# A transformer block on one core: in the FFN's second product, the sixth product's right blocks are loaded ahead of the last two left operands

## What is computed

```
FFN_HIDDEN = int(math.ceil(8 * D_MODEL / 3 / 256)) * 256        # 2816

def swiglu(h, w_in_ffn, w_out_ffn):
    g, u = jnp.split(h @ w_in_ffn, 2, axis=-1)
    return (jax.nn.silu(g) * u) @ w_out_ffn

xl = xl + gt2 * swiglu(modulate(rms_norm(xl, g_ffn[l]), sh2, sc2), w_ffn_in[l], w_ffn_out[l])
...
return rms_norm(xl, g_final)
```

## Time and profile before

| | us |
|---|---|
| three timed runs | 1302.32, 1302.75, 1305.46 |
| median | 1302.75 |
| the profiled execution's own time | 1297.05 |
| its span in the trace | 1295.2 |
| TensorE busy | 1255.0 (97% of the span) |
| DVE, ACT busy | 923.3 (71%), 652.1 (50%) |

### The profile page before, as it was taken

The page is one execution under the profiler, slowest core; times in us unless marked ns, Lnnn a source line. Parts: engine busy times, 40 slices in busy tenths (PEclk is TensorE's granted clock), DMA queues, the critical chain, the costliest instruction groups (busy, mean ns, idle before and its releaser), DMA issues. The chain is left out here.

```text
span 1295.2 us, 22622 instructions
## 1 busy us (share of the span) xinstructions
PE 1255.0 (97%) x7808; PEld 656.8 (51%) x7808; DVE 923.3 (71%) x1546; ACT 652.1 (50%) x1240; POOL 305.3 (24%) x301
## 2 busy tenths in 40 slices
PE   8999999999898999999999999999999999999997
PEld 1564656444675666665455444444444444444443
DVE  3779986686688999974356976666666676576387
ACT  2532123544697999993125554444454444312225
POOL 0100000121132789960001233333322230000001
PEclk9999999999999999999999999999999999999999
DMA  9627702052240131011112222222223204997953
GB/s 372 241 89 301 292 33 65 1 163 66 74 174 1 34 130 32 0 34 49 49 49 82 65 85 71 71 75 81 89 89 89 74 31 135 325 341 270 358 194 131
DMA packets 106709, 158.89 MB, mean 123 GB/s; under 512 B 8209, under 2 KB 67089, under 8 KB 104849
## 3 DMA queue, kind: packets, MB, share of 16 engines
q1 hardware_dynamic: 106640, 158.00, 35.6%
HBM read 135.95 MB, written 19.93 MB: 120 GB/s over the span
## 5 line engine op out<-in xcount | busy, mean ns | idle before, releaser
L1105 PE MATMUL PS<-arena 128*128 128x512 f16 (+9 forms) x7208 | 1206.6, 327 | 21.3 <-DMA arena<-in_w_mod 7.2
L1105 PEld LDWEIGHTS PS<-arena 128*128 128x128 f16 (+3 forms) x7208 | 605.9, 102 | 592.9 <-issue 47.5
L2708 DVE SCALAR_TENSOR_TENSOR arena<-arena 128x512 f16<-128x512 f32 x148 | 120.9, 823 | 76.7 <-ACT arena L2010 76.7
L2010 ACT ACTIVATE arena<-arena 128x512 f16<-128x512 f32 x140 | 87.6, 629 | 130.4 <-PE PS L1105 130.4
L2615 DVE TENSOR_REDUCE arena<-PS 128x1 f32<-128x512 f32 (+1 forms) x160 | 105.5, 680 | 9.8 <-PE PS L1105 9.8
L2122 ACT ACTIVATE arena<-arena 128x512 f16<-128x512 f32 x77 | 48.2, 629 | 127.4 <-DVE arena L2856 72.8
L1946 ACT ACTIVATE arena<-PS 128x512 f16<-128x512 f32 x144 | 91.3, 634 | 2.6 <-PE PS L1105 2.1
L980 POOL TENSOR_TENSOR arena<-arena 128x2 f32<-128x2 f32 (+1 forms) x18 | 21.1, 1173 | 260.9 <-DVE arena L2467 260.9
L1020 POOL TENSOR_TENSOR arena<-arena 128x512 f16<-128x512 f32 x64 | 74.0, 1158 | 23.7 <-ACT arena L1949 22.4
L1072 POOL TENSOR_TENSOR arena<-arena 128x512 f32<-128x512 f32 x20 | 26.4, 1322 | 222.8 <-DMA arena<-in_w_ffn_in 212.0
L2635 DVE TENSOR_TENSOR arena<-PS,arena 128x512 f16<-128x512 f32 x96 | 65.4, 682 | 8.3 <-ACT PS L1949 8.3
(11 more groups left out here) (199 smaller groups left out, 1111.2 us busy)
## 6 DMA issues: line engine op xcount, KB each, us to landing
arena<-in_w_ffn_out SPq DMA_DIRECT2D x121, 256.0 KB, 5.0
arena<-in_w_mod SPq DMA_DIRECT2D x24, 1024.0 KB, 7.3
arena<-in_w_ffn_in SPq DMA_DIRECT2D x88, 256.0 KB, 2.9
arena<-in_w_in SPq DMA_DIRECT2D x9, 1024.0 KB, 5.3
left_operands<-arena SPq DMA_DIRECT2D x33, 256.0 KB, 2.2
arena<-left_operands SPq DMA_DIRECT2D x3, 2816.0 KB, 14.9
arena<-lay_bias SPq DMA_DIRECT2D x4, 1536.0 KB, 8.9
arena<-in_x SPq DMA_DIRECT2D x2, 2048.0 KB, 14.7
```

Of the source, the lines that this page charges most:

```text
L1105: return pe.matmul(out, lhsT, rhs, start=start, stop=stop, skip_group_check=True)
L2010: act.activation(aS[n % RING][:, 0], weight_block(p, b), ACT.Copy, scale=WS).then_inc(blk_hi, 1)
L2708: dve.scalar_tensor_tensor(dst[:, 1], src, WS, dst[:, 0], ALU.mult, ALU.subtract).then_inc(blk_lo, 1)
```

## The change

P3's eleven right blocks (steps 5 x KQ to 6 x KQ - 1) are loaded ahead of the left operands. The first eight, as many as there are raw slots, come ahead of S4; the other three come between S4 and A22, which is now the last. SP waits for the stored sums and P6's splits at its old place, behind S4. Nothing else is changed.

```
             load_fo(3 * KQ + 4, 5 * KQ)
             sp.wait_ge(fo_mm, 4 * (DOWN.index("P6") + 1))
             load_x2("C21")
+            load_fo(5 * KQ, 5 * KQ + FO_RAW)
             load_left(KEPT_OUT.index("S4"))
             for j in range(4):
                 sp.wait_ge(t2_out[j], 16 * len(range(j, KQ, 4)))
             sp.wait_ge(fo_lo, 3 * KQ)
+            load_fo(5 * KQ + FO_RAW, 6 * KQ)
             load_left(KEPT_OUT.index("A22"))
-            load_fo(5 * KQ, 7 * KQ)
+            load_fo(6 * KQ, 7 * KQ)
```

## The result

| | before | after |
|---|---|---|
| median of 20 timed runs, us | 1302.18 | 1305.79 |
| lowest to highest | 1298.60 to 1305.46 | 1302.87 to 1310.36 |
| profiled execution, us | 1297.05 | 1302.87 |
| its span | 1295.2 | 1301.1 |

The ratio is 1.003 with a 95% interval of 1.0021 to 1.004: the changed kernel is slower by 3.6 us. One or two executions of each of four kernels further down took 1340 to 4666 us, and the ratios and medians leave them out. The prediction had 3.8 us more and a time of 1306.5. The sum was right. Two of its terms were far too small, and their errors cancelled.

The account below looks back on a forecast made before the run. The prediction took TensorE, busy 97% of the span, to bound the kernel. Its terms 3.9 - 1.3 + 1.2 = +3.8 us, added to the median of 1302.75, gave 1306.5 us, with a range of 1302.0 to 1310.0.

Parts of the forecast that it names:

- wait for A22: At P3's start TensorE, ready at 1229.3, waits until about 1233.2 for A22 on the count shared with S4: +3.9 us.
- clock behind it: After TensorE's wait at P3 the granted clock falls to 0.57 over 4 us: +1.2 us, bounds 0 and 1.7.
- waits that go: P4's waits for DVE's splits vanish because DVE is earlier and has 7 us of cover: -1.3 us.
- so its waits cost 1.3 us: In the kernel before, P4 would end undisturbed at 1286.5 but ends at 1287.77, a loss of 1.3 us.
- ready at 1229.3: TensorE is ready for P3's first matmul at 1229.3, 3.5 us after A22's old landing at 1225.8.
- TensorE doesn't wait there: In the kernel before, TensorE has no wait at P3's first matmul, which stands at 1229.3.
- the second product was the same there: The timed runs' median lies 5.7 us above the profiled execution, with the second product the same, so the difference is added.
- price per block: Each of P3's blocks takes 0.66 us of the DMA engines, so eleven land A22 7.3 us later.
- SP's issue backs up: Rival: the three blocks between S4 and A22 hold SP, A22 is issued at about 1226; +5.6 us, 1308.4; 13%.
- P4's waits stay: Rival: DVE isn't earlier after all, so P4 still waits for splits; +5.1 us, 1307.9; 7%.
- the clock doesn't fall: Rival: TensorE's clock stays up after the wait at P3; +2.6 us, 1305.3; 22%.
- A22 comes in time: Rival: A22 lands by 1229.3, so TensorE doesn't wait at P3 and only -1.3 us is left, 1301.4; 8%.

Follow-up runs that it names:

- before, again: The kernel before, with no edit, run once more for a second trace: ratio 1.000 (0.9987 to 1.0014), median 1301.77 us.
- before, own count: The kernel before, with its order of loads kept but A22 taken off S4's semaphore count: ratio 0.9994 of before (0.9981 to 1.0008).
- changed, again: The changed kernel, with no edit, run once more for a second trace: ratio 1.0025 of before (1.0012 to 1.0038).
- three blocks last: The changed kernel with A22 loaded ahead of P3's last three blocks, shared count kept: ratio 1.0019 of before (1.0006 to 1.0031), median 1303.46 us.
- changed, own count: The changed kernel with A22 off S4's semaphore count, so P3 waits for S4 alone and P4 for A22: ratio 0.9961 of before (0.9946 to 0.9976).
- the same, again: The changed order with A22 off S4's count, run once more on another chip: ratio 0.9963 of before (0.9949 to 0.9977).
- S4 first, own count: The changed kernel with A22 off S4's count and S4 loaded ahead of all eleven blocks: ratio 0.9965 of before (0.9953 to 0.9977).
- wait kept warm: The changed kernel with 30 extra matmuls on zero weights ahead of P3's wait: ratio 1.0009 of before (0.9993 to 1.0026).

## Why the prediction was right, and which terms were not

The mechanism was right in the steps that the traces can show. A22 lands behind the eleven blocks, 20.9 and 20.6 us behind C21 (21.0 by the prediction's count). P3 waits for an operand that it doesn't read, the clock falls (already within the wait, not only behind it), DVE is earlier, P4's gaps go, and the end is TensorE's.

The sizes of the terms:

| term | predicted | measured |
|---|---|---|
| wait for A22 | +3.9 | +7.6 and +6.9 (two traces) |
| clock behind it | +1.2 (0 to 1.7) | +1.3 and +1.5; 2.7 behind the gap of 3.3 us |
| waits that go | -1.3 | -5.1 and -4.8 (the ratios 0.9961 and 0.9963 of the order without a wait); 4.9 lost in the second trace of before |
| sum | +3.8 | +3.6 |

The failed step is in the first part, "so its waits cost 1.3 us", and in the third, "ready at 1229.3" against a landing worked out from the same trace. So is "TensorE doesn't wait there", of P3's start: it waited 1.03 and 2.02 us there in the two other traces of this order. All of them take one distance from one trace: C21 landed 17.2 us ahead of P3's due time. In the other traces it was (lost is TensorE's end less the due time less 57.2 us; where there is no gap, the due time is counted back from the end):

| trace | C21 lands | P3 due | distance | gaps of TensorE in P3 and P4 | lost |
|---|---|---|---|---|---|
| before | 1212.1 | 1229.3 | 17.2 | 0.7 | 1.3 |
| before, again | 1216.7 | 1231.1 | 14.4 | 4.1 | 4.9 |
| before, own count | 1218.1 | 1231.5 | 13.4 | 3.0, and the clock | 5.3 |
| changed | 1214.3 | 1227.6 | 13.3 | 7.6, and the clock | 9.0 |
| changed, again | 1217.7 | 1231.3 | 13.6 | 6.9, and the clock | 8.5 |
| three blocks last | 1215.0 | 1231.8 | 16.8 | 3.3, and the clock | 6.2 |
| changed, own count | 1216.2 | 1232.1 | 15.9 | none | 0 |
| the same, again | 1217.5 | 1231.1 | 13.6 | none | 0 |
| S4 first, own count | 1218.4 | 1231.2 | 12.8 | none | 0 |
| wait kept warm | 1211.7 | 1229.4 | 17.7 | none, 30 more matmuls | 6.5 (these matmuls) |

A shorter distance makes both kernels slower. In the order of before P3's and P4's splits are late, and the loss rises from 1.3 to 4.9 and 5.3 us. With the shared count and the new order the gap is the time from C21 to A22 less the distance (20.9 - 13.3, 20.6 - 13.6, 20.1 - 16.8). Hence each of the two terms was 3 to 4 us too small, and their difference held. That the errors have opposite signs follows from the one distance in both; that they are so nearly equal was luck, for the prediction didn't foresee it. The losses give the result again: 9.0 and 8.5 less 4.9 is 4.1 and 3.6 us.

The prediction noted that its profiled execution was 5.7 us below the median and then said that the second product was the same there. This was the sentence to test. The spans of the two traces of before differ by 5.5 us: 3.6 are lost in P3 and P4, and by 1.8 TensorE reaches P3 later, which was lost ahead of the second product, as it has no gap from 1000 to P3 in either trace. Why C21 lands at another distance from run to run was not tried; the waits for P5's and P7's blocks ahead of it differ (DVE's idle time before the sums of P6, P5 and P7 is 30.6 us in the first trace of before and 32.4 in the second), and that is all the traces say.

The wait's own range, 3.6 to 5.5, missed both traces of the changed kernel. The range for the whole, 1302.0 to 1310.0, held. The price per block is less firm than one trace made it look: over the five traces with eleven blocks and S4 ahead of A22 it is 20.6 to 22.2 us from C21 to A22, which with operands of 7.0 and 6.7 leaves 0.63 to 0.77 us per block, and 0.80 where eight stood ahead of it. The 0.60 us that the prediction set beside its 0.66 lies below all of these. Two slips of arithmetic changed nothing: its shares for slower add up to 45% and more (25, 13, 7), not 43%, and A22's landing by the terms of the rival with SP's issue is 1226.1 + 1.2 + 6.7 = 1234.0, not 1234.4; no row stands behind its 1.2 and 1.3.

Of the rivals, that SP's issue backs up didn't happen (A22 was issued at 1218.10 and landed 17.1 us later, of which its own transfer takes 6.7, so it stood ten microseconds in the queue); that P4's waits stay is out; that the clock doesn't fall is out; and that A22 comes in time is out.

## What to carry to other kernels

Before a load is moved behind others, look at who waits on its semaphore, not only at who reads its data: with a shared count the first reader waits for the last load. An order of loads and the waits that hang on it are one edit; here each alone was worth nothing or less, and both together 0.4%. And take a wait from more than one execution where the profiled one lies outside the timed ones: its slack is then not the usual slack.

## What the runs showed of the chip

How long the granted clock stays low behind a wait was not what the trace of before had led me to expect. A gap of 1.03 us left it at 1.00, one of 2.02 us was followed by (0.13 + 0.30) x 8 = 3.4 us at 1.2 GHz, and with gaps of 3.3, 6.9 and 7.6 us it was low for 6.8 us each time. With a long wait most of the low stretch falls into the wait and costs 1.3 to 1.5 us; with the gap of 3.3 us it falls behind it and costs 2.7. So the price of the clock was not bounded by 1.7 us, and a shorter wait can pay more for it than a longer one.

Short gaps close together are not the same as one wait. In the second trace of before three gaps of 1.37, 0.50 and 1.19 us stand within 5 us, and the clock stays at 1.00 (busy time of PE, PEld, DVE, ACT, POOL, then the granted clock, the DMA share and GB/s):

```profile
1264.00:1268.00 4.00, 2.29 (x10) 0.70 (x8) 2.82 (x5) 1.50 (x3) 0.00 (x0) 1.00 0.83 277
1268.00:1272.00 4.00, 2.61 (x11) 0.92 (x12) 3.11 (x8) 2.44 (x7) 0.00 (x0) 1.00 0.01 3
```

TensorE is busy for 2.29 and 2.61 us of 4 there. The prediction had taken bursts of 3.02 and 2.09 us, after which the clock fell, as its sign that a wait of 4 us would cost clock; here bursts like these were followed by no fall. One trace stands behind each of the gaps named here, so whether the same gap always does the same stays open.
